# First norm of a hybrid decoder layer on one core: how the mean, the root and the split of h are made, and the order of the first query tile

## The reference

```python
z = x @ w_in                                   # q, k, v of two attentions, indexer, two gates
a = diff_attention(z); o = sparse_attention(z) # with paged caches for the sample tokens
merged = sigmoid(ga) * (a @ w_a_up) + sigmoid(gb) * (o @ w_b_up)
h = layer_norm(ALPHA * x + merged @ w_out, ln1_g, ln1_b)
y = layer_norm(ALPHA * h + peer(h), ln2_g, ln2_b)

def layer_norm(x, g, b):
    mu = mean(x); var = mean((x - mu) ** 2)
    return (x - mu) * rsqrt(var + 1e-5) * g + b

def peer(t):                                   # 8 heads, 16384 single-neuron experts
    q = t @ peer_wq                            # 1024 -> 8 x 2 x 128
    s = q . sub_keys                           # 16 sets of 128 scores per token
    top-16 of each, top-16 of their sums, softmax
    return sum over chosen experts of gelu(t . u_e) * gate_e * v_e
```

## Time and profile before

| | |
|---|---|
| median of 3 runs | 1203.47 us (1202.66 to 1206.82) |
| profiled execution | 1202.06 us, its span 1200.4 us |
| PE busy | 1135.0 us, 95% of the span |
| DVE busy | 823.3 us, 69% |
| ACT busy | 538.0 us, 45% |
| POOL busy | 457.7 us, 38% |
| mean granted TensorE clock | 0.98 of 2.4 GHz |

### The profile page before, as it was taken

The page is one execution under the profiler, slowest core; times in us unless marked ns, Lnnn a source line. Parts: engine busy times, 40 slices in busy tenths (PEclk is TensorE's granted clock), DMA queues, the critical chain, the costliest instruction groups (busy, mean ns, idle before and its releaser), DMA issues.

```text
span 1200.4 us, 22934 instructions
## 1 busy us (share of the span) xinstructions
PE 1135.0 (95%) x7693; PEld 1027.9 (86%) x7693; DVE 823.3 (69%) x1825; ACT 538.0 (45%) x959; POOL 457.7 (38%) x243
## 2 busy tenths in 40 slices
PE   7998897898799999999999999999999999999997
PEld 7997675588699998989999999998888888878886
DVE  4446926556699999965666677745666668657666
ACT  4334335333335766765444444443333334334433
POOL 1010325042467999996666666665000003000000
PEclk9999998999899999999999999999999999999998
DMA  6773577335143454444443333344555558445552
GB/s 242 257 278 151 172 247 272 107 105 175 54 140 126 172 175 151 173 166 142 138 140 140 139 133 133 138 150 162 194 193 193 193 192 325 168 156 188 181 193 88
DMA packets 55824, 205.39 MB, mean 171 GB/s; under 512 B 6336, under 2 KB 6336, under 8 KB 55392
## 3 DMA queue, kind: packets, MB, share of 16 engines
q1 hardware_dynamic: 48960, 177.30, 42.7%
q0 software_dynamic: 6528, 27.20, 6.7%
q10 hardware_dynamic: 288, 0.31, 0.1%
HBM read 201.41 MB, written 3.38 MB: 171 GB/s over the span
## 4 chain that ended last, share of the span: by engine, by line
PE 80%; issue 7%; POOL 5%; DVE 5%; ACT 2%; DMA 1%; POOLq 0%; DVEq 0%; ACTq 0%
PE psum L1875 29%; PE psum L1819 9%; PE psum L1814 9%; PE psum L1815 8%; PE psum L1548 5%; PE psum L1849 5%; PE psum L1549 4%; PE psum L1552 4%; POOL w_lo L588 4%; PE psum L1793 1%; PE psum L1751 1%; PE psum L1747 1%; DMA arena<-k_cache_dram 1%; PE psum L1748 1%; PE psum L1532 1%
## 5 line engine op out<-in xcount | busy, mean ns | idle before, releaser
L588 POOL TENSOR_TENSOR w_lo<-ring,w_hi 128x1024 fp32r<-128x1024 f32 x128 | 335.4, 2628 | 115.6 <-ACT w_hi L812 115.3
L1814 PE MATMUL psum<-h_hi,w_hi 128*128 128x272 f32 x1024 | 261.6, 294 | 0.0
L1815 PE MATMUL psum<-h_lo,w_hi 128*128 128x256 f32 x1024 | 255.0, 281 | 0.0
L863 ACT ACTIVATE w_hi<-ring 128x1024 fp32r<-128x1024 f32 x128 | 135.6, 1061 | 215.9 <-PE psum L1875 208.2
L812 ACT ACTIVATE w_hi<-ring 128x1024 fp32r<-128x1024 f32 x128 | 135.5, 1059 | 165.5 <-PE psum L1815 130.6
L1814 PEld LDWEIGHTS psum<-h_hi,w_hi 128*128 128x128 f32 x1024 | 192.8, 188 | 0.3 <-issue 0.2
L1815 PEld LDWEIGHTS psum<-h_lo,w_hi 128*128 128x128 f32 x1024 | 192.9, 188 | 0.0
L1875 PE MATMUL psum<-w_hi,cells_hi 128*128 128x512 f32 x512 | 159.7, 393 | 2.7 <-ACT w_hi L863 2.7
L1407 DVE TENSOR_TENSOR w_lo<-ring,w_hi 128x1024 fp32r<-128x1024 f32 x128 | 157.1, 1227 | 2.8 <-ACT w_hi L863 2.8
L1875 PE MATMUL psum<-w_hi,cells_lo 128*128 128x512 f32 x512 | 158.5, 391 | 0.0
L1819 PE MATMUL psum<-h_hi,w_lo 128*128 128x264 f32 x1024 | 147.2, 286 | 8.8 <-POOL w_lo L588 8.7
(11 more groups left out here) (300 smaller groups left out, 1796.9 us busy)
## 6 DMA issues: line engine op xcount, KB each, us to landing
ring<-experts_u_dram SPq DMA_DIRECT2D x128, 512.0 KB, 3.2
ring<-experts_v_dram SPq DMA_DIRECT2D x128, 512.0 KB, 3.2
ring<-weights_dram SPq DMA_DIRECT2D x78, 512.0 KB, 3.5
arena<-k_cache_dram POOLq DMA_DIRECT2D x16, 576.0 KB, 6.0
arena<-v_cache_dram POOLq DMA_DIRECT2D x16, 512.0 KB, 7.6
kv_out_dram<-arena POOLq DMA_DIRECT2D x1, 2244.0 KB, 8.6
arena<-alibi_dram POOLq DMA_DIRECT2D x1, 1664.0 KB, 8.6
xt<-x_t_dram SPq DMA_DIRECT2D x2, 528.0 KB, 6.0
```

Of the source, the lines that this page charges most:

```text
L588: pool.tensor_tensor(halves_of(w_lo, k, D), raw, halves_of(w_hi, k, D), ALU.subtract)\
L863: act.activation(halves_of(w_hi, k, D), raw, ACT.Copy).then_inc(S["v_hi_made"], 1)
L1814: pe.matmul(out[:, 0:WIDE], part(hi, c, P), h_hi[:, at:at + WIDE], start=(c == 0), stop=False)
L1815: last = pe.matmul(out[:, 0:TP], part(hi, c, P), h_lo[:, at:at + TP], start=False, stop=False)
```

## The change

The norm. The running sum takes chunks 0 to 6 only; the mean comes from two products with ones into one PSUM bank, of the sum and of the last chunk. ACT takes the root straight from PSUM (scale 1/D, epsilon as a bias column that DVE sets at the start), and DVE then makes the reciprocal. All eight chunks are scaled on DVE by one operation each (times gain, times the reciprocal root). ACT adds the bias and rounds into h_hi, chunk by chunk; DVE makes h_lo from the scaled chunk, the bias and h_hi. No f32 copy of h is written, and POOL has no part in the norm.

The order around it. On ACT the first query weight tile is converted ahead of the last up tile. On PE the first four query tiles are written out ahead of the loop, and the very first takes high and low weights with h_hi of every chunk first, then the high weights with h_lo.

```diff
@@ POOL
-            def norm_scale(src):
-                pool.wait_ge(S["ln_root"], 1)
-                for k in range(0, DC, 2):
-                    pool.tensor_tensor(src[:, k, :], src[:, k, :], ln_root, ALU.mult).then_inc(S["ln_scaled"], 1)
...
             wq_low(0, 0)
             wq_low(0, 1)
-            norm_scale(pre)
@@ ACT
-            for m in range(DC + 2, 2 * DC):
+            for m in range(DC + 2, 2 * DC - 1):
                 act.wait_ge(S["tiles_done"], UP_AT + m - 1)
                 up_high(0, m)
...
-                act.wait_ge(S["ln_recip"], 1)
-                act.activation(ln_root, ln_root, ACT.Sqrt).then_inc(S["ln_root"], 1)
-                for k in range(0, DC, 2):
-                    act.wait_ge(S["ln_scaled"], k // 2 + 1)
-                    act.activation(dst[:, k, :], src[:, k, :], ACT.Identity, bias=par[:, b + k:b + k + 1],
-                                   scale=par[:, g + k:g + k + 1]).then_inc(S["ln_even"], 1)
-
-                    act.wait_ge(S["ln_even"], k // 2 + 1)
-                    act.wait_ge(S["ln_odd"], k // 2 + 1)
-                    act.activation(token_pair(h_hi, k), xt[:, k * T:(k + 2) * T].rearrange("p (c t) -> p c t", c=2), ACT.Copy)\
+                act.wait_ge(S["ln_stat"], 2)
+                act.wait_ge(S["eps_ready"], 1)
+                act.activation(ln_root, psum[:, LN_BANKS[1], 0:T], ACT.Sqrt, bias=eps[:, 0:1], scale=1.0 / D)\
+                    .then_inc(S["ln_root"], 1)
+                for k in range(DC):
+                    act.wait_ge(S["ln_scaled"], k + 1)
+                    act.activation(token_part(h_hi, k), src[:, k, :], ACT.Identity, bias=par[:, b + k:b + k + 1])\
                         .then_inc(S["h_hi_made"], 1)
...
             wq_high(0, 0)
+            act.wait_ge(S["tiles_done"], OUT_AT + DC - 2)
+            up_high(0, 2 * DC - 1)
             wq_high(0, 1)
@@ DVE
+            dve.memset(eps[:, :], EPS).then_inc(S["eps_ready"], 1)
...
-                if n:
+                if 0 < n < DC - 1:
...
-                dve.wait_ge(S["ln_stat"], 2)
-                chain(dve.tensor_scalar(ln_root, psum[:, LN_BANKS[1], 0:T], 1.0 / D, EPS, ALU.mult, ALU.add))
-                dve.reciprocal(ln_root, ln_root).then_inc(S["ln_recip"], 1)
                 dve.wait_ge(S["ln_root"], 1)
-                for k in range(1, DC, 2):
-                    chain(dve.tensor_tensor(src[:, k, :], src[:, k, :], ln_root, ALU.mult))
-                    dve.tensor_scalar(dst[:, k, :], src[:, k, :], par[:, g + k:g + k + 1], par[:, b + k:b + k + 1],
-                                      ALU.mult, ALU.add).then_inc(S["ln_odd"], 1)
...
+                dve.wait_ge(S["ln_centred"], DC)
+                chain(dve.reciprocal(ln_root, ln_root))
+                for k in range(DC):
+                    dve.scalar_tensor_tensor(src[:, k, :], src[:, k, :], par[:, g + k:g + k + 1], ln_root,
+                                             ALU.mult, ALU.mult).then_inc(S["ln_scaled"], 1)
+                for k in range(DC):
+                    dve.wait_ge(S["h_hi_made"], k + 1)
+                    dve.scalar_tensor_tensor(token_part(h_lo, k), src[:, k, :], par[:, b + k:b + k + 1], token_part(h_hi, k),
+                                             ALU.add, ALU.subtract).then_inc(S["h_lo_made"], 1)
@@ PE
-            pe.wait_ge(S["chunks_summed"], DC - 1)
-            pe.matmul(psum[:, LN_BANKS[0], 0:T], ones, ln_sum, start=True, stop=True).then_inc(S["ln_stat"], 1)
+            pe.wait_ge(S["chunks_summed"], DC - 2)
+            pe.matmul(psum[:, LN_BANKS[0], 0:T], ones, ln_sum, start=True, stop=False)
+            pe.wait_ge(S["out_free"], 4 + DC)
+            pe.matmul(psum[:, LN_BANKS[0], 0:T], ones, pre[:, DC - 1, :], start=False, stop=True).then_inc(S["ln_stat"], 1)
...
+            def first_query(out, hi, lo):
+                pe.wait_ge(S["wq_hi_made"], 1)
+                pe.wait_ge(S["wq_lo_made"], 1)
+                for c in range(DC):
+                    pe.wait_ge(S["h_hi_made"], c + 1)
+                    pe.matmul(out, part(hi, c, P), token_part(h_hi, c), start=(c == 0), stop=False)
+                    pe.matmul(out, part(lo, c, P), token_part(h_hi, c), start=False, stop=False)
+                for c in range(DC):
+                    pe.wait_ge(S["h_lo_made"], c + 1)
+                    last = pe.matmul(out, part(hi, c, P), token_part(h_lo, c), start=False, stop=(c == DC - 1))
+                return last
...
+            queries(0, True)
+            with pe.Fori(1, HC // 4) as i:
+                queries(i, False)
```

More of the change, by code:

```diff
@@ L136, in build_program @@
             pad_zero pad_filled out_sample_ready rms_square rms_recip rms_root rms_spread up_b_filled up_b_free
-            up_a_free merged out_free ln_stat ln_centred ln_square ln_recip ln_root ln_scaled ln_even
-            ln_odd q_evac score_filled score_free wq_hi_made wq_lo_made h_hi_made h_lo_made u_hi_made
+            up_a_free merged out_free ln_stat ln_centred ln_square ln_root ln_scaled eps_ready
+            q_evac score_filled score_free wq_hi_made wq_lo_made h_hi_made h_lo_made u_hi_made
             u_hi_used u_lo_made u_done gelu_done route_ready route_exp gates_normed route_filled
@@ L162, in build_program @@
         small = region("small", SMALL)
+        eps = region("eps", 1)
         x_hi = rounded("x_hi", "ht", 0, ROW - PITCH + WIDE)
@@ L755, in _, with norm @@
                         .then_inc(S["merged_hi_made"], 1)
-            for m in range(DC + 2, 2 * DC):
+            for m in range(DC + 2, 2 * DC - 1):
                 act.wait_ge(S["tiles_done"], UP_AT + m - 1)
                 up_high(0, m)
-            def norm(src, dst, g, b):
+            def norm(src, g, b):
                 for k in range(DC):
@@ L784, in _ @@
             wq_high(0, 0)
+            act.wait_ge(S["tiles_done"], OUT_AT + DC - 2)
+            up_high(0, 2 * DC - 1)
             wq_high(0, 1)
             act.wait_ge(S["params_loaded"], 16)
-            norm(pre, h, P_LN1G, P_LN1B)
+            norm(pre, P_LN1G, P_LN1B)
             act.sem_inc(S["q_evac"], 2)
@@ L820, in gelu @@
                                psum[:, 4 + k, 0:TP], ACT.Gelu).then_inc(S["gelu_done"], 1)
-            act.wait_ge(S["h_lo_made"], DC // 2)
+            act.wait_ge(S["h_lo_made"], DC)
             high_part(0, 0)
@@ L1253, in norm @@
                     dve.tensor_tensor(src[:, k, :], src[:, k, :], ln_mean, ALU.subtract).then_inc(S["ln_centred"], 1)
-                dve.wait_ge(S["ln_stat"], 2)
-                chain(dve.tensor_scalar(ln_root, psum[:, LN_BANKS[1], 0:T], 1.0 / D, EPS, ALU.mult, ALU.add))
-                dve.reciprocal(ln_root, ln_root).then_inc(S["ln_recip"], 1)
                 dve.wait_ge(S["ln_root"], 1)
-                for k in range(1, DC, 2):
-                    chain(dve.tensor_tensor(src[:, k, :], src[:, k, :], ln_root, ALU.mult))
-                    dve.tensor_scalar(dst[:, k, :], src[:, k, :], par[:, g + k:g + k + 1], par[:, b + k:b + k + 1],
-                                      ALU.mult, ALU.add).then_inc(S["ln_odd"], 1)
[L1263 to L1267, removed]
+                dve.wait_ge(S["ln_centred"], DC)
[7 more added lines that the diff above has]
+                                             ALU.add, ALU.subtract).then_inc(S["h_lo_made"], 1)
+            norm(pre, P_LN1G, P_LN1B)
             low, beside = h_lo[:, TP:T], h_hi[:, T:WIDE]
-            dve.wait_ge(S["h_lo_made"], DC // 2)
+            dve.wait_ge(S["h_lo_made"], DC)
             dve.tensor_copy(bass.AP(beside.tensor, beside.offset, [list(beside.ap[0]), [PITCH, DC], [1, TS]]),
@@ L1787, in _, with queries @@
             pe.sem_inc(S["score_filled"], 2)
-            with pe.Fori(0, HC // 4) as i:
+            def first_query(out, hi, lo):
[9 more added lines that the diff above has]
+                return last
+            def queries(i, first):
                 def sub_scores(k):
@@ L1799, in _ @@
                     pe.wait_ge(S["q_evac"], i * 4 + k + 1)
-                    project_parts(psum[:, k % 2, 0:T], halves_of(wq_hi, k, D), halves_of(wq_lo, k, D), (h_hi, h_lo),
-                                  S["wq_hi_made"], S["wq_lo_made"], i * 4 + k + 1,
-                                  S["h_lo_made"] if k == 0 else None, 2).then_inc(S["tiles_done"], 1)
+                    out, hi, lo = psum[:, k % 2, 0:T], halves_of(wq_hi, k, D), halves_of(wq_lo, k, D)
+                    if first and k == 0:
+                        first_query(out, hi, lo).then_inc(S["tiles_done"], 1)
+                    else:
+                        project_parts(out, hi, lo, (h_hi, h_lo), S["wq_hi_made"], S["wq_lo_made"], i * 4 + k + 1)\
+                            .then_inc(S["tiles_done"], 1)
                     if k:
@@ L1820, in u_block @@
                 last.then_inc(S["u_done"], 1)
-            pe.wait_ge(S["h_lo_made"], DC // 2 + 1)
+            pe.wait_ge(S["h_lo_made"], DC + 1)
             with pe.Fori(0, BEFORE_ROUTES // RING) as i:
```

## The result

| | before | after |
|---|---|---|
| median of 20 runs | 1206.31 us (1201.6 to 1210.61) | 1200.17 us (1196.23 to 1204.4) |
| ratio | | 0.9953, 95% interval 0.9941 to 0.9966 |
| profiled execution | 1202.06 us | 1196.23 us |
| span | 1200.4 us | 1194.5 us |

The change makes the kernel faster by 0.47%, about 5.7 us; 5.2 was forecast. The median, 1200.17, lies 1.9 us over the forecast of 1198.3 and inside its range, since the kernel before also came out higher in these twenty runs than in its first three (1206.31, then 1203.47). The saving came out near the forecast and two of its three terms did, but the third did not. The profiled execution after the change is the fastest of its twenty, so the two profiles show the stages and not the typical total.

The account below looks back on a forecast made before the run. PE was taken as the bound, busy 1135.0 of 1200.4 us, so its idle places could be won. 1.10 + 0.41 + 3.7 = 5.2 us saved gave 1196.9 us profiled, 1198.3 us on the median, range 1196.2 to 1201.6.

Parts of the forecast that it names:

- Mean: First norm: two ones-products, the first run while DVE makes the eighth chunk, bring the mean 1.10 us earlier.
- The cost of 0.10 by a late evacuation: Last output tile: POOL holding up DVE delays its evacuation, taking 0.10 of the 1.20 us won on the mean.
- Root: First norm: Sqrt straight from PSUM, then the reciprocal, with no table load added; 0.41 us won.
- Scaling, split, first query tile: From the first scaling to the second query tile on PE: 9.68 us becomes 6.0, 3.7 us won.
- PE starts at X + 1.2: First query tile: PE starts 1.2 us after X, the start of the first scaling, and follows ACT's h_hi.
- The upper bound (0.43): New DVE operations in scaling and split: 0.43 us each if they don't overlap, 1.4 us less won over 16.
- a pitch over 0.40: Scaling and split on DVE: a pitch above 0.40 us would show the prediction wrong; 0.344 was taken.
- rival b: PE's idle gap lowers its clock, and a half-clock second query tile costs 1.4 us; saving 3.8, 1199.7 us, chance 0.14.
- Rival (a): Last output tile: POOL gets the shared port before DVE's up_low, so the mean wins 0.08; 1199.4 us, chance 0.18.
- Rival (c): PE's longer program misses code fetches at the expert loop's 12 backward jumps, 26 us lost; 1224 us, chance 0.03.
- Rival (d): Stage behind is paced by DVE or loads, hiding half; 3.6 us or less, about 1201.5 us, chance 0.10.

Follow-up runs that it names:

- token_early: Changed kernel with ACT handing out the two free-PSUM-bank tokens ahead of the norm, not behind it; 0.9934 of the kernel before, 0.9957 in a second set.
- token_warm: As token_early, with six extra ones-products, results unused, keeping PE busy in the gap before the first query tile; 0.9949 of the kernel before.
- peel_only: Kernel before with only the first four query tiles written out on PE ahead of the loop; ratio 0.9990 (0.9974 to 1.0006).

## Why the prediction was right, and where it was not

- *Mean*, 1.10 forecast, 1.25 measured. The step was right, and the pattern of DVE and POOL came as drawn. POOL's first low part began 6.55 us ahead of the last evacuation (285.25 and 291.80; 6.54 by the forecast's 288.29 and 294.83). DVE's up_low began at 287.96, 0.17 ahead of POOL's second. The cost of 0.10 by a late evacuation did not appear: PE's last pass over the last output tile and the evacuation start 1.13 us apart (290.67 and 291.80), where it was 1.14. What I had not seen is that the two edits take away the same 0.72 us.
- *Root*, 0.41 forecast, 0.40 measured: Sqrt 0.48 (0.49), no table load, reciprocal 1.80.
- *Scaling, split, first query tile*: 3.7 forecast, 0.8 measured in two profiles and 1.9 in the third. The step that failed is that PE starts at X + 1.2 and so follows ACT. It starts at X + 3.42, because I listed ACT's and DVE's products as what PE waits for and not the tokens for PSUM banks. The trace of before had the row, on PE's weight load at the start of that tile, and I read only the matmul's:

```profile
310.77 0.29 PEld L1548 LDWEIGHTS psum<-h_hi,wq_hi 128*128 128x128 f32 x1 [8.56 <-ACTq L789]
```

  There the token and the first h_lo came within about 0.1 us of each other (ACT's last h_hi, behind whose issue the token stands, began at 310.56, and the first h_lo ended at 310.67), and the token cost nothing. With h_lo no longer the first thing needed, it was next. token_early puts the step right: X + 1.19, and X + 6.84 where the sum had 6.0.
- The remaining 0.84 is the pitch on DVE. I took 0.344 from a subtraction of two tensors. With a gain column beside two tensors one operation takes 0.484 and the pitch is (3.32 - 0.48)/7 = 0.406; 16 of them make 1.0 us. The upper bound (0.43) held it, but the prediction had named a pitch over 0.40 as a sign that it is wrong; the 16 operations took 6.55 us and not 5.6. ACT's pitch, 0.41 forecast, is (3.35 - 0.50)/7 = 0.41.
- *Clock* (rival b): half clock over the whole first tile in two of three profiles and into the second by 0.34 and 0.10 us. As forecast the gap was enough to lower it. That it would be hidden behind ACT and DVE failed with the token: a PE that starts late holds the tile itself, at up to 1.05 us (X + 8.87 against 7.82). In token_early it is hidden, as token_warm shows.
- *Rival (a)* did not happen. *Rival (c)* is excluded by peel_only: from 0.9974 to 1.0006 there is no room for a loss of 20 us. *Rival (d)*: behind the stage nothing was lost, 881.6 against 882.4.
- The total, 5.7 against 5.2, agrees by luck: the terms as measured in the first two profiles come to 1.25 + 0.40 + 0.81 = 2.5, less the 0.34 of the second tile, and the rest came from a surplus that was in no term and that goes mostly with the clock of the executions (3.0 us at one clock). A right total is no proof of its terms.

## What to carry to other kernels

Before a consumer is moved forward, list everything its engine waits for at that place, free-buffer tokens included, and look where each is given in its giver's program: a token that stands behind a long block there comes with the end of the block. Read the releaser of the weight load as well as that of the matmul, and look for waits that end within 0.2 us of the one you remove. Compare a stage by its marks in several profiles before taking a difference of medians for its size, and price a DVE operation by a row with the same kinds of operands.

The version with the token ahead of the norm has the shortest stage of those run, by 1.0 to 2.4 us under the changed kernel. In time it is 0.9934 and 0.9957 of the kernel before, and these intervals overlap those of the changed kernel's 0.9953 and 0.9956. At one clock it gains 5.5 and 4.2 us and the changed kernel 3.0 and 2.2.

## What the runs showed of the hardware

- A scalar_tensor_tensor on DVE over 128x264 with a column and a second tensor in SBUF takes 0.484 us, one every 0.41, where a subtraction of two tensors takes 0.43, one every 0.344.
- Where DVE and POOL hold each other up, they took turns. In the kernel before, POOL had a low part running when a DVE product was issued at 404.53; that product took 4.39 us, where another DVE operation of the same size just before it (L1330) took 2.29. POOL's next low part, issued at 406.73 as its last one ended, took 4.42 and not 2.39: DVE, which had waited, went first, and then POOL. All six operations of L1334 took 4.36 to 4.39 us, each behind a low part of POOL, so none shows what it takes alone.

```profile
404.53 4.39 DVE L1334 TENSOR_TENSOR work<-work 128x2048 f32<-128x2048 f32 x1
406.73 4.42 POOL L588 TENSOR_TENSOR w_lo<-ring,w_hi 128x1024 fp32r<-128x1024 f32 x1
```

- The changed kernel ran its first query tile at half clock in all of it (two profiles) or in two thirds of its time (one), and the stage was 1.2 to 1.4 us longer with the first. In the old order three profiles had two thirds, and peel_only, which runs the same operations, had all of it and a stage 1.4 us longer.
